# Which weight strips stay in SBUF, and at which beat a block's mixer, attention and selection run, in a two-layer PEER trunk

## The reference

```python
ue = u[e]; ve = v[e]                       # e: token x 8 heads x 16 experts
a = gelu(einsum('thkd,td->thk', ue, xb)) * softmax(best scores)
y = einsum('thk,thkd->td', a, ve)
```

## Time and profile before

| what | value |
|---|---|
| median of 3 runs | 2903.66 us (2902.95 to 2907.32) |
| the profiled execution | 2907.78 us |
| its span, first to last instruction | 2906.0 us |
| busy: TensorE, VectorE, ScalarE, GpSimd | 78%, 75%, 41%, 43% |
| moved by DMA | 1170.26 MB, mean 403 GB/s |

### The profile page before, as it was taken

The page is one execution under the profiler, slowest core; times in us unless marked ns, Lnnn a source line. Parts: engine busy times, 40 slices in busy tenths (PEclk is TensorE's granted clock), DMA queues, the critical chain, the costliest instruction groups (busy, mean ns, idle before and its releaser), DMA issues.

```text
span 2906.0 us, 27009 instructions
## 1 busy us (share of the span) xinstructions
PE 2257.9 (78%) x7300; PEld 1200.6 (41%) x7300; DVE 2185.6 (75%) x5166; ACT 1183.3 (41%) x3457; POOL 1263.8 (43%) x1049
## 2 busy tenths in 40 slices
PE   8678777687877877787787878878778777876667
PEld 6535443354423544243343434433444434432222
DVE  2687768875878757796688876988679876887664
ACT  2144324343443433344444463445534453433333
POOL 0155335443454433444434543354434454345555
PEclk9799899999998998899898998999899998998989
DMA  6499999999999999999999999999999999999998
GB/s 270 174 410 421 413 359 420 421 420 413 404 420 422 420 389 415 421 422 421 421 391 416 422 421 421 388 413 421 421 418 398 420 421 420 404 420 422 421 422 351
DMA packets 170816, 1170.26 MB, mean 403 GB/s; under 512 B 19668, under 2 KB 19928, under 8 KB 36136
## 3 DMA queue, kind: packets, MB, share of 16 engines
q0 software_dynamic: 147456, 1073.81, 89.4%
q1 hardware_dynamic: 23208, 94.74, 8.3%
HBM read 1164.28 MB, written 4.19 MB: 402 GB/s over the span
## 4 chain that ended last, share of the span: by engine, by line
DMA 29%; DVE 14%; PE 10%; issue 6%; POOL 3%; ACT 3%; POOLq 0%; DVEq 0%; ACTq 0%
DMA ring<-in_uv,pick 27%; PE acc L1716 5%; DVE ring L1093 5%; POOL ring L666 3%; PE ps L1511 3%; DVE side L1084 1%; DMA xc<-h 1%; DMA stream<-in_strips 1%; ACT diag L1369 1%; DVE arena L968 1%; DVE arena L949 1%; DVE arena L950 1%; ACT coef L1361 1%; DVE arena L1039 1%; DVE arena L1043 1%
## 5 line engine op out<-in xcount | busy, mean ns | idle before, releaser
L666 POOL DMA_INDIRECT ring<-in_uv,pick x1024 | 1259.3, 1230 | 1616.5 <-PE acc L1716 1084.1
L1716 PE MATMUL acc<-ring,diag 128*128 128x512 f32 x2988 | 1523.6, 652 | 474.6 <-ACT diag L1369 474.1
L1093 DVE CUSTOM_DVE_ANT_0 ring<-ring,h_now 128x1024 f32<-128x1024 f32 x1024 | 1236.0, 1223 | 494.5 <-DMA ring<-in_uv,pick 483.2
L1716 PEld LDWEIGHTS acc<-ring,diag 128*128 128x128 f32 x2988 | 576.0, 204 | 1286.0 <-ACT diag L1369 719.4
L1358 ACT ACTIVATE gelu<-dots 128x1 f32<-128x1 f32 x1024 | 206.1, 201 | 1263.2 <-DVE dots L1093 1261.8
L1084 DVE SCALAR_TENSOR_TENSOR side<-ring,coef,side 128x1024 f32<-128x1024 f32 x270 | 346.1, 1282 | 18.9 <-ACT coef L1361 18.9
L1361 ACT ACTIVATE coef<-gate,gelu 128x1 f32<-128x1 f32 x1024 | 301.9, 295 | 33.2
L1369 ACT ACTIVATE diag<-ident,coef 128x128 f32<-128x128 f32 x747 | 300.1, 402 | 28.2 <-PE acc L1716 3.9
L1511 PE MATMUL ps<-resident,actT 128*128 128x256 f32 x896 | 217.5, 399 | 16.5 <-ACT actT L1170 16.5
L1511 PEld LDWEIGHTS ps<-resident,actT 128*128 128x128 f32 x896 | 175.7, 200 | 59.4 <-ACT actT L1170 18.1
L1478 PE MATMUL ps<-actT,stream 128*128 128x128 f32 x960 | 125.6, 292 | 27.4 <-DMA stream<-in_strips 26.6
(11 more groups left out here) (196 smaller groups left out, 1439.2 us busy)
## 6 DMA issues: line engine op xcount, KB each, us to landing
stream<-in_strips SPq DMA_DIRECT2D x102, 512.0 KB, 9.3
resident<-in_strips SPq DMA_DIRECT2D x18, 1024.0 KB, 12.3
ring<-in_uv,pick POOLq DMA_INDIRECT x1024, 14.9
ring<-in_strips SPq DMA_DIRECT2D x9, 1024.0 KB, 19.7
arena<-in_keys SPq DMA_DIRECT2D x8, 512.0 KB, 7.8
xc<-in_x SPq DMA_DIRECT2D x4, 512.0 KB, 6.2
h<-arena SPq DMA_DIRECT2D x4, 512.0 KB, 11.5
xc<-h SPq DMA_DIRECT2D x4, 512.0 KB, 7.8
```

What stands on the lines that cost most here:

```text
L666: pool.indirect_dma_start(ring[:, n % SLOTS, :], None, tables[layer], bass.IndirectOffsetOnAxis(ap=pick[:, col:col + 1], axis=0),).then_in ...
L1093: dve.tensor_tensor_reduce(ring[:, slot, 0:D], ring[:, slot, 0:D], h_now[:], 1.0, 0.0, ALU.mult, ALU.add, dots[:, slot:slot + 1]).then_inc ...
L1716: m = pe.matmul(acc[:, b * 512:(b + 1) * 512], diag[:, turn % 4, :], ring[:, slot, D + b * 512:D + (b + 1) * 512], start=(r == 0 and i == ...
```

## The change

Which 9 strips are resident becomes a list for each layer (`KEPT`), and the passing ones (`PASSING`) are spread over the order: in layer 0 strips 0, 1, 2, 3, 4, 6, 8, 10, 12, 14 and 19 pass, in layer 1 strips 0, 4, 5 and 12. The numbers of resident and passing strips stay 9 and 11, and 9 and 4. `left` (q and k of layer 0) learns to wait for and free cuts. On SyncE's queue the sub-keys now stand behind a block's last strip, layer 1's bias and late resident strips move into the loop over strips, and 4 resident strips instead of 5 come ahead. At the opening the strips are loaded in the order of their numbers, into `resident` or `ring` (14 and 19, which pass through `stream`, last). The beats in `AT` of the gated and the window mixer are all placed anew (those of `act` in step with the ones shown), and `AT["first"]` moves `q1`, `k0`, `k1` alone. `VECTOR` has 34 side sums a stage for `gla` (37 before) and 30 for `swa` (34 before); in the first three rounds 2 and 3, where there were 9 and 10. The wait of GpSimd's first gathers for `pq1` goes, since ring slots hold earlier strips.

```diff
 RESIDENT = 9
 CUTS = 2
 CUT = 8 // CUTS
-STREAMED = tuple(s - RESIDENT for s in STRIPS)
+KEPT = ((5, 7, 9, 11, 13, 15, 16, 17, 18), (1, 2, 3, 6, 7, 8, 9, 10, 11))
+PASSING = tuple(tuple(n for n in range(STRIPS[layer]) if n not in KEPT[layer]) for layer in range(2))
+STREAMED = tuple(len(p) for p in PASSING)
 
 PARTS = 4
 PART = HEADS_P // PARTS
-SAYS = ({11: "r", 15: "y", 16: "pq0", 17: "pq1", 18: "pq2", 19: "pq3"},
-        {8: "y", 9: "pq0", 10: "pq1", 11: "pq2", 12: "pq3"})
-DONE = [[SAYS[layer].get(n) for n in range(RESIDENT, STRIPS[layer])] for layer in range(2)]
+SAYS = ({1: "q", 3: "k", 19: "pq3"}, {4: "kv", 12: "pq3"})
+DONE = [[SAYS[layer].get(n) for n in PASSING[layer]] for layer in range(2)]
 FREED = [[e for event in events for e in [None] * (CUTS - 1) + [event]] for events in DONE]
-GAIN_AT = (13 - RESIDENT, 10 - RESIDENT)
-AHEAD, AHEAD_AT, REST_AT = 5, 10, 5
-KEYS_AT = (16 - RESIDENT, 10 - RESIDENT)
+GAIN_AT = (PASSING[0].index(14), PASSING[1].index(12))
+AHEAD, AHEAD_AT, REST_AT = 4, 10, 5
...
     "gla": (
-        ((1, 4, 7),) * 3 + ((0, 2, 4, 6),) + ((1, 4, 7),) * 2 + ((0, 2, 4, 6),) + ((1, 3, 5, 7),) +
-        ((0, 3, 6),) + ((2, 6),) + ((1, 4),) + ((2, 6),) + ((4,),) + ((),) * 3),
+        ((1,),) + ((),) + ((4,),) + ((0, 2, 4, 6),) + ((1, 3, 5, 7),) * 2 + ((0, 2, 4, 6),) + ((1, 3, 5, 7),) +
+        ((0, 2, 4, 6),) + ((1, 3, 5, 7),) + ((1, 4, 7),) + ((4,),) + ((),) * 4),
     "swa": (
-        ((1, 4, 7),) * 2 + ((0, 2, 4, 6),) + ((0, 4),) + ((1, 5),) + ((0, 3, 6),) + ((2, 6),) +
-        ((1, 4, 7),) * 2 + ((2, 6),) + ((1, 3, 5, 7),) + ((0, 3, 6),) + ((),) * 4),
+        ((1,),) + ((),) + ((3, 6),) + ((0, 4),) + ((1, 4, 7),) + ((0, 3, 6),) + ((1, 4, 7),) * 2 + ((0, 2, 4, 6),) +
+        ((0, 2, 4, 6),) + ((1, 4, 7),) + ((2, 6),) + ((),) * 4),
 }
...
     "gla": {
-        "pe": {"hT": 7, "q0": 12, "q1": 24, "k0": 29, "k1": 38, "v0": 43, "v1": 45, "v2": 49, "v3": 52, "attn": 56,
-               "r0": 56, "r1": 56, "r2": 60, "upd": 62, "r3": 62, "o0": 64, "o1": 64, "oT": 69, "out0": 71,
-               "out1": 73, "out2": 76, "out3": 79, "h2T": 84, "pq0": 84, "sc0": 86, "pq1": 88, "sc1": 90, "pq2": 94,
-               "sc2": 94, "pq3": 105, "sc3": 118},
...
-        "dve": {"var": 8, "h": 9, "absx": 43, "b": 47, "qd": 53, "mask": 57, "state0": 65, "state1": 69, "o": 69,
-                "x2": 84, "var2": 85, "h2": 85, "pick00": 91, "pick01": 93, "pick02": 93, "pick03": 93, "pick04": 93,
-                "pick05": 93, "pick06": 97, "pick07": 98, "pick10": 98, "pick11": 101, "pick12": 101, "pick13": 101,
-                "pick14": 102, "pick15": 107, "pick16": 107, "pick17": 107, "pick20": 112, "pick21": 112,
-                "pick22": 112, "pick23": 114, "pick24": 114, "pick25": 115, "pick26": 121, "pick27": 127, "pick30": 1,
-                "pick31": 1, "pick32": 13, "pick33": 13, "pick34": 13, "pick35": 16, "pick36": 24, "pick37": 24},
+        "pe": {"hT": 7, "q0": 11, "q1": 15, "k0": 18, "k1": 22, "v0": 26, "v1": 28, "v2": 31, "v3": 33, "attn": 38,
+               "r0": 40, "r1": 43, "r2": 46, "upd": 49, "r3": 50, "o0": 54, "o1": 55, "oT": 61, "out0": 64,
+               "out1": 68, "out2": 72, "out3": 76, "h2T": 82, "pq0": 83, "sc0": 86, "pq1": 88, "sc1": 91, "pq2": 94,
+               "sc2": 97, "pq3": 104, "sc3": 112},
...
+        "dve": {"var": 8, "h": 9, "absx": 26, "b": 30, "qd": 35, "mask": 40, "state0": 52, "state1": 58, "o": 59,
+                "x2": 79, "var2": 81, "h2": 82, "pick00": 89, "pick01": 90, "pick02": 90, "pick03": 91, "pick04": 92,
+                "pick05": 92, "pick06": 95, "pick07": 96, "pick10": 97, "pick11": 98, "pick12": 99, "pick13": 100,
+                "pick14": 101, "pick15": 102, "pick16": 106, "pick17": 107, "pick20": 109, "pick21": 110,
+                "pick22": 111, "pick23": 112, "pick24": 114, "pick25": 115, "pick26": 121, "pick27": 124,
+                "pick30": 1, "pick31": 2, "pick32": 4, "pick33": 6, "pick34": 9, "pick35": 12, "pick36": 18,
+                "pick37": 20},
...
     "swa": {
-        "pe": {"hT": 4, "q0": 13, "q1": 16, "q2": 18, "q3": 22, "kv": 25, "qT": 32, "s0": 34, "s1": 38, "pT0": 42,
-               "s2": 42, "o0": 49, "pT1": 51, "s3": 51, "o1": 58, "pT2": 61, "o2": 64, "pT3": 67, "o3": 68, "oT": 70,
-               "out0": 75, "out1": 82, "out2": 87, "out3": 87, "h2T": 92, "pq0": 93, "sc0": 95, "pq1": 96, "sc1": 99,
-               "pq2": 100, "sc2": 111, "pq3": 112, "sc3": 120},
...
-        "dve": {"var": 5, "h": 6, "qvar": 29, "qn": 32, "rope": 32, "m0": 37, "m1": 43, "m2": 50, "m3": 57, "o": 72,
-                "x2": 93, "var2": 93, "h2": 94, "pick00": 101, "pick01": 101, "pick02": 101, "pick03": 101,
-                "pick04": 101, "pick05": 102, "pick06": 102, "pick07": 102, "pick10": 105, "pick11": 105,
-                "pick12": 105, "pick13": 105, "pick14": 105, "pick15": 109, "pick16": 109, "pick17": 113,
-                "pick20": 113, "pick21": 113, "pick22": 118, "pick23": 118, "pick24": 118, "pick25": 119,
-                "pick26": 120, "pick27": 126, "pick30": 0, "pick31": 0, "pick32": 0, "pick33": 1, "pick34": 9,
-                "pick35": 17, "pick36": 26, "pick37": 27},
+        "pe": {"hT": 5, "q0": 10, "q1": 13, "q2": 15, "q3": 17, "kv": 19, "qT": 26, "s0": 28, "s1": 32, "pT0": 36,
+               "s2": 37, "o0": 42, "pT1": 44, "s3": 46, "o1": 51, "pT2": 54, "o2": 58, "pT3": 60, "o3": 64, "oT": 67,
+               "out0": 70, "out1": 74, "out2": 78, "out3": 82, "h2T": 89, "pq0": 90, "sc0": 93, "pq1": 95, "sc1": 98,
+               "pq2": 100, "sc2": 104, "pq3": 108, "sc3": 115},
...
+        "dve": {"var": 5, "h": 6, "qvar": 23, "qn": 26, "rope": 26, "m0": 31, "m1": 35, "m2": 41, "m3": 50, "o": 67,
+                "x2": 86, "var2": 88, "h2": 89, "pick00": 96, "pick01": 96, "pick02": 97, "pick03": 97,
+                "pick04": 98, "pick05": 99, "pick06": 102, "pick07": 102, "pick10": 103, "pick11": 104,
+                "pick12": 104, "pick13": 105, "pick14": 106, "pick15": 107, "pick16": 110, "pick17": 111,
+                "pick20": 113, "pick21": 114, "pick22": 114, "pick23": 115, "pick24": 116, "pick25": 117,
+                "pick26": 122, "pick27": 126, "pick30": 0, "pick31": 1, "pick32": 2, "pick33": 4, "pick34": 8,
+                "pick35": 12, "pick36": 18, "pick37": 20},
     },
     "first": {
-        "pe": {"hT": 34, "q0": 37, "q1": 39, "k0": 43, "k1": 46, "v0": 54, "v1": 54, "v2": 60, "v3": 60, "attn": 61,
...
+        "pe": {"hT": 34, "q0": 37, "q1": 41, "k0": 45, "k1": 49, "v0": 54, "v1": 54, "v2": 60, "v3": 60, "attn": 61,
...
+        def passing(prep, n):
+
+            return n in PASSING[prep.layer]
...
             def load_kept_ahead(prep):
 
-                said_by(sp, "pe", before(prep), "v")
+                said_by(sp, "pe", before(prep), "r")
...
             def load_streamed(prep):
-                if prep.layer == 1:
-
-                    said_by(sp, "pe", prep, "o3")
-                    sp.dma_start(bias_out, b_out).then_inc(bias_loaded, 16)
                 opening = prep.first and prep.layer == 0
-                if opening:
-                    for n in range(SLOTS):
-                        sp.dma_start(ring[:, n, :], strips[0][RESIDENT + n]).then_inc(ring_loaded[n], 16)
                 for n in range(STREAMED[prep.layer]):
-                    if n == GAIN_AT[prep.layer]:
+                    if n == GAIN_AT[prep.layer] + opening:
+
+                        if prep.layer == 1:
+                            if prep.first:
+                                load_kept_rest(prep)
+
+                            said_by(sp, "pe", prep, "o3")
+                            sp.dma_start(bias_out, b_out).then_inc(bias_loaded, 16)
 
                         said_by(sp, "pe", prep, "oT")
                         if prep.layer == 0:
 
                             said_by(sp, "dve", prep, "state1")
                         sp.dma_start(ffn_gain, gain_ffn[prep.layer:prep.layer + 1, :]).then_inc(gain_loaded, 16)
-                    if n == KEYS_AT[prep.layer]:
-
-                        said_by(sp, "pe", prep, "y")
-                        sp.dma_start(keysT, (keys0, keys1)[prep.layer]).then_inc(keys_loaded, 16)
...
-                                     strips[prep.layer][RESIDENT + n, :, c * CUT * STRIP:(c + 1) * CUT * STRIP])\
+                                     strips[prep.layer][PASSING[prep.layer][n], :, c * CUT * STRIP:(c + 1) * CUT * STRIP])\
                           .then_inc(slot_loaded[c], 16)
 
+                said_by(sp, "pe", prep, "y")
+                sp.dma_start(keysT, (keys0, keys1)[prep.layer]).then_inc(keys_loaded, 16)
+
             def preps(prep, after):
-                if prep.first:
-                    load_kept_rest(prep)
                 load_streamed(prep)
                 if prep.layer == 0 and after.layer == 1:
...
-            for n in range(RESIDENT):
-                load_kept(Prep("gla", 0), n)
+            def load_opening(begin, end):
```

(59 more changed lines are left out.)

## The result

The changed kernel takes 2917.75 us (median of 5 runs, 2913.91 to 2920.13) against 2903.66 (five runs of the kernel before beside them): a ratio of 1.0038, 95% interval 1.0025 to 1.005. It is slower by 0.4%, where 0.9% faster was forecast. The two profiled executions stand closer together (2913.91 and 2907.78 us) than the medians, since the one of after is the fastest of its runs and the one of before lies above its median; so the traces can account for 6 us, and the size of the rest rests on the timed runs.

The account below looks back on a forecast made before the run. DMA bytes bound the kernel, at a 421 GB/s plateau; seven dips, 39.3 us, were within reach. 15.8 + 13.3 - 2 = 27 us off the median 2903.7 gave 2877 us, range 2858 to 2898.

Parts of the forecast that it names:

- Fewer side sums: 26 side sums move from VectorE to TensorE, seven in a stage's first three rounds; claimed to fit, term 0.
- The cover of 12 us: Lateness of the dot products that the ring's queue of gathers hides at no cost; taken as 12 us, range 5 to 12.5.
- Steps of `choose` spread: Four layer-1 selection dips, 17.4 us: spreading the steps cuts lateness from 17.1 to 8.2 us, winning 13.3.
- D: Theory formed after four runs, not forecast: passing strips fill engine-limited stretches where gathers could not start; removing them costs their bytes.
- Passing strips spread: Three dips at the end of layer-0 preparations, 21.9 us: fewer strips passing there wins 15.8 (8.5, 2.8, 4.5).
- the lower bound that I named: Layer-0 dips: about half, 11 us, is won if the first-stage table keeps its own bunch of selection steps.
- Strips at the front: Stages 1 and 2, beats 11 to 31: TensorE waits 6.1 us for early strips, mostly hidden; 2 us lost together.
- the bound beside it: Early strips in stages 1 and 2: without the 2.5 us per strip, waits are 18 us and 15 us are lost.
- SyncE, opening: SyncE's reordered queue and the opening's new load order: term 0 each, the opening within 2.5 us either way.
- The slower rival: Stage's first quarter: strips land in 12 us or more, TensorE is the clock, 52 us lost, 2929; chance 0.08.
- The mark set down: Sign of being wrong: new dips below 400 GB/s stand 40 to 90 us after a stage's start.

Follow-up runs that it names:

- e1: Changed kernel with the side sums (`VECTOR`) of the kernel before put back: 2906.47 us, 1.0009 of before.
- e6: Kernel before with the new beats (`AT`) and, in rounds 0 to 2 only, the new side sums; old strips: 2930.59 us, 1.0086 of before.
- e3: Kernel before with the new beats (`AT`) alone, strips and side sums as before: 2901.74 us, 0.9982 of before.
- e4: Kernel before with the new side sums (`VECTOR`) alone, strips and beats as before: 2920.92 us, 1.0050 of before.
- e2: Kernel before with the new spread of passing strips and SyncE's new order alone, beats and side sums as before: 2926.34 us, 1.0069 of before.
- b3: Changed kernel with the side sums of before and stage 0's table spread: 2910.50 us, 1.0011 of before.
- b1: Kernel before with the new beats, the window mixer's head later and stage 0 spread; strips and side sums as before: 2898.57 us, 0.9972 of before.

## Why the prediction was wrong

- **"Fewer side sums", term 0**: failed, the first cause. The mechanism was in its bound (seven picks, 12.3 us late if TensorE's time is full), and in stages 3 to 6 its time is full: 20.9 of 48.1 us go to the mixer's strips. I added up round 1 for `gla` alone. The same sum for `swa`, whose `q0`, `q1` and `q2` all stand in that round, is 8 x 1.75 + 3 x 4.2 = 26.6 us against 19.9 + 2.5: it does not fit. I set the lateness against the queue's cover and let it go. With the strips and beats of after it costs 11 us (after against e1; 8 by the ratios), with the strips of before 29 (e6 against e3), with the beats of before too 15 (e4).
- **The cover of 12 us**: failed. Of the burst I took all bytes for gathers. The queues view of the same 27.1 us of before says otherwise:

```profile
DMA packets 1585, 9.43 MB, mean 348 GB/s; under 512 B 177, under 2 KB 177, under 8 KB 691
...
q0 software_dynamic: 1003, 7.31, 71.5%
q1 hardware_dynamic: 580, 2.11, 19.3%
```

2.11 MB are two strips, 5.0 us at 421 GB/s. They hid that part of the 12.4, and the gathers 7.4. Even that is too much for e6's fronts, which lost 9.5 us of a lateness put at 12.3. What the ring hides at the start of a stage stays open.
- **"Steps of `choose` spread", 13.3 us**: the step is right and its gain was taken back twice. With the strips of before the four selections lose 4 us instead of 19 (e3), but the same beats, mixer and attention earlier, lose 12 more in beats 0 to 47, so 2 us are left. With the strips spread the selections lose 19.1 us instead of 17.4. Two steps failed: I took the dips for losses that can be won one by one, and I counted strips only as waits of TensorE, never as bytes that fill a stretch limited by engines. Of the four strips only `pq3` still passes, so 7.5 us of filling are taken from each of four selections. D is shown by before against e2 and by e3 against e1.
- **"Passing strips spread", 15.8 us**: the two places of stages 1 and 2 won 9.9 where 7.3 was foreseen, but the strips were not needed for it: e3 has the old ones and runs at 419 in both. Stage 0 won nothing of 8.5. The waits went as written (x2 4.1 us) and the loss moved behind 430 us. Half of the stage's bunch stayed, the lower bound that I named, but b3, which spreads it with these strips, is no faster than e1; with the strips of before it helps (b1).
- **Strips at the front, 2 us**: the waits were right. TensorE waited 6.9 us for strips from 515 to 580 us (L1466 5.6, L1522 1.3), 6.1 foreseen from a landing of 9.5. The Trainium skill ("DMA: Bandwidth & Descriptors", Anatomy of one DMA) led to an estimate of 3.2 us for a landing, by which there would be none; the row was the better guide. e1, with these strips and the old sides, ran at 408 in stage 1 (515 to 600) and 413 in stage 2 (860 to 945), 2.6 and 1.6 us; e3, with the old strips, at 421 and 410, so 2.2 of the 4.2 are there without these strips. About 2 are left, the size of the term. In the bound beside it the five waits add up to 17, not 18.
- **SyncE, opening**: 0 foreseen, 0.9 measured in the opening.
- **The slower rival** had the place right (a stage's first quarter, TensorE as the clock) and the mechanism wrong: it asked for strips that land in 12 us, and in stages 3 to 6 picks and projections sufficed. The mark set down, new dips below 400 GB/s 40 to 90 us after a stage's start, is what four of the six fronts show; the other two stand at 401.

What stays open besides: some 8 us of the 14 between the medians, which the profiled executions don't contain, and why closing a dip in stages 3 to 6 opens another.
